# Even projection: the sample group's rows as fp32 products in four PSUM bands, summed by a 0/1 product

## What is computed

```python
def even_mixer(h, pos, R0, w_in, w_out, q_gain, k_gain, attend):
    b, T = h.shape[:2]
    qr, kr, vr, gr, qa, ka, va, qi, ki, wi = _split(h @ w_in, EVEN_SPLITS)
...
def reference(...):
...
        np_ = rmsnorm(xp, norm_mix[l])
        ns_ = rmsnorm(xs, norm_mix[l])
```

## Time and profile before

| | |
|---|---|
| median of three runs | 3229.15 us (3225.47 to 3239.33) |
| the profiled execution, its own time | 3233.79 us |
| its span in the trace | 3231.7 us |
| TensorE busy | 2905.4 us, 90% of the span |
| VectorE busy | 1493.0 us, 46% |
| ScalarE busy | 730.5 us, 23% |
| GpSimd busy | 314.2 us, 10% |
| mean granted clock of TensorE | 0.928 |

### The profile page before, as it was taken

The page is one execution under the profiler, slowest core; times in us unless marked ns, Lnnn a source line. Parts: engine busy times, 40 slices in busy tenths (PEclk is TensorE's granted clock), DMA queues, the critical chain, the costliest instruction groups (busy, mean ns, idle before and its releaser), DMA issues. The chain is left out here.

```text
span 3231.7 us, 38976 instructions
## 1 busy us (share of the span) xinstructions
PE 2905.4 (90%) x16549; PEld 2663.2 (82%) x16549; DVE 1493.0 (46%) x2021; ACT 730.5 (23%) x1166; POOL 314.2 (10%) x287
## 2 busy tenths in 40 slices
PE   8889996638879899999999979958799999999998
PEld 7757775627539899999999979836599999999997
DVE  4789994678313433322332345248423332332333
ACT  3533330235321311111111032132312111111110
POOL 1022222512130100000000010015001000000000
PEclk9989998858989899999999989957699999999999
DMA  5022223143132121121121021010202111112111
GB/s 163 7 87 90 95 73 125 48 141 106 48 123 66 46 59 40 40 60 40 40 59 40 14 44 47 22 33 1 62 21 65 40 53 46 40 43 57 40 40 67
DMA packets 210737, 188.18 MB, mean 58 GB/s; under 512 B 22843, under 2 KB 164415, under 8 KB 210425
## 3 DMA queue, kind: packets, MB, share of 16 engines
q1 hardware_dynamic: 204033, 164.36, 16.9%
q0 software_dynamic: 6528, 21.23, 2.2%
HBM read 152.25 MB, written 33.50 MB: 57 GB/s over the span
## 5 line engine op out<-in xcount | busy, mean ns | idle before, releaser
L1929 DVE TENSOR_TENSOR xt<-ps,xt 128x1056 f32<-128x1056 f32 x176 | 221.0, 1256 | 205.7 <-PE ps L1713 205.7
L1713 PE MATMUL ps<-ffn_high,f_whG 128*128 128x352 f32 x1056 | 230.0, 326 | 13.2 <-DVE ffn_low L1643 7.8
L1713 PE MATMUL ps<-f_hidh,f_whD 128*128 128x352 f32 x1056 | 229.6, 326 | 9.9 <-DVE f_wlD L1908 9.9
L1713 PE MATMUL ps<-ffn_low,f_whG 128*128 128x352 f32 x1056 | 229.1, 325 | 0.0
L1713 PE MATMUL ps<-f_hidh,f_wlD 128*128 128x352 f32 x1056 | 228.9, 325 | 0.0
L1713 PE MATMUL ps<-ffn_low,f_whU 128*128 128x352 f32 x1056 | 228.7, 324 | 0.0
L1713 PE MATMUL ps<-f_hidl,f_whD 128*128 128x352 f32 x1056 | 228.4, 324 | 0.0
L1713 PE MATMUL ps<-ffn_high,f_whU 128*128 128x352 f32 x1056 | 227.8, 324 | 0.0
L1713 PE MATMUL ps<-ffn_high,f_wlG 128*128 128x352 f32 x1056 | 227.6, 324 | 0.0
L1713 PE MATMUL ps<-ffn_high,f_wlU 128*128 128x352 f32 x1056 | 226.6, 323 | 0.0
L728 PE MATMUL ps<-pe_wh,even_high 128*128 128x512 f32 (+1 forms) x504 | 200.2, 397 | 13.3 <-POOL pe_wl L760 13.3
(11 more groups left out here) (538 smaller groups left out, 4837.5 us busy)
## 6 DMA issues: line engine op xcount, KB each, us to landing
pe_w<-in_w_in_even_dram SPq DMA_DIRECT2D x7, 2048.0 KB, 8.3
proj<-pe_out SPq DMA_DIRECT2D x56, 256.0 KB, 2.0
ht_even<-in_w_gate_dram SPq DMA_DIRECT2D x22, 512.0 KB, 5.1
ht_even<-in_w_up_dram SPq DMA_DIRECT2D x22, 512.0 KB, 6.3
ht_even<-in_w_down_dram SPq DMA_DIRECT2D x22, 512.0 KB, 3.9
ht_odd<-in_w_gate_dram SPq DMA_DIRECT2D x22, 512.0 KB, 5.1
ht_odd<-in_w_up_dram SPq DMA_DIRECT2D x22, 512.0 KB, 6.3
ht_odd<-in_w_down_dram SPq DMA_DIRECT2D x22, 512.0 KB, 3.9
```

What stands on the lines that cost most here:

```text
L1713: last = pe.matmul(g.ps[0:out_rows, b0 + c, 0:THIRD], lhs, rhs[:, c * THIRD:(c + 1) * THIRD], start=(first and n == 0), stop=(final and n ...
L1929: dve.tensor_tensor(xv, g.ps[:, 3 * (m % 2):3 * (m % 2) + 3, 0:THIRD], xv, ALU.add).then_inc(added, 1)
```

## The change

The sample rows leave the product of three fp32r passes. For each strip, the 8 slices of the sample rows are multiplied with the gained weights in `pe_w` as plain fp32 products; slice k goes to PSUM band k % 4 (32 partitions each) of one bank, so each band sums two slices. ScalarE copies the whole bank to a new tile `pe_bands`, and one more plain fp32 product with a constant 0/1 matrix (`fold`, 128 by 32, a one where row i and column j have i % 32 = j) adds the four bands into partitions 0 to 31 of the same bank. The ninth unit moves from the last to the third place in the order of a strip; its products are issued between the full units 0 and 1, and the fold between 1 and 2. The load of the next strip's weights also waits for the products of the sample rows. The fp32 tile of the sample columns now lives as long as the halves.

```diff
--- before.py
+++ after.py
@@ -119,6 +119,7 @@
     head = 2 * ((q % 16) // 4) + (q % 32) // 16
     put("head_idx", (head[:, None] == np.arange(IH)[None, :]) * 1.0)
     put("page_row", i[:, None] * 1.0)
+    put("fold", (i[:, None] % NS == np.arange(NS)[None, :]) * 1.0)
 
     cnt = np.stack([1.0 / np.minimum(np.arange(PPAST) + 1, 2 ** (g + 1)) for g in range(4)])
     put("pool_head", np.tile(cnt.reshape(1, -1), (P, 1)))
@@ -198,6 +199,7 @@
                 with ExitStack() as normed:
                     halves(normed, "even", "right")
                     g.inverse = room(normed, "even_inverse", [P, TILES], F32, "right")
+                    g.x_sample = room(normed, "x_sample", [P, KD, NS], F32, "right")
                     g.score = room(att, "score", [P, 6, SEQ])
                     g.score_s = room(att, "score_s", [NS, KEYS])
                     stage_front(g)
@@ -288,7 +290,7 @@
         scaled = relu[:, :, :].rearrange("p s n -> p (s n)")[:, 0:2 * T].rearrange("p (s n) -> p s n", s=2)
         x_last = early[:, 2 * SEQ:4 * SEQ].rearrange("p (k n) -> p k n", k=2)
         x_places = (((0, g.score[:, 0:4, :]),), ((0, g.score[:, 4:6, :]), (2, x_last)))
-        x_sample = g.room(st, "fr_x_sample", [P, KD, NS])
+        x_sample = g.x_sample
         block = st.enter_context(nc.Block())
         key_rows = g.ins["cache_kidx"][0].rearrange("n p d -> (n p) d")
         units = [(t, h) for t in range(2, SMP) for h in range(IH)]
@@ -685,16 +687,25 @@
 
     nc = g.nc
     projected, copied = g.sem("pe_projected"), g.sem("pe_copied")
+    banded, bands_read, folded = g.sem("pe_banded"), g.sem("pe_bands_read"), g.sem("pe_folded")
     w_in, w_rounded, w_split = g.sem("pe_weights"), g.sem("pe_rounded"), g.sem("pe_split")
     stored = g.slot_sems("pe_stored", 4)
     found, replaced = g.sem("pe_found"), g.sem("pe_replaced")
+
+    order = [(m, t) for m in range(EVEN_TM) for t in (0, 1, SMP, *range(2, SMP))]
+    place = {unit: n for n, unit in enumerate(order)}
     with ExitStack() as st:
         w = g.room(st, "pe_w", [P, KD, 512])
         wh = g.room(st, "pe_wh", [P, 2, KD, 512], F32R)
         wl = g.room(st, "pe_wl", [P, 2, KD, 512], F32R)
         out = g.room(st, "pe_out", [P, 4, 512])
+        bands = g.room(st, "pe_bands", [P, 2, 512])
         best = g.room(st, "pe_best", [P, 8])
         block = st.enter_context(nc.Block())
+
+        def tiles_before(m, t):
+
+            return SMP * m + t
 
         @block.sync
         def _(sp):
@@ -703,32 +714,59 @@
                              .rearrange("(k p) n -> p k n", p=P)).then_inc(w_in, 16)
 
             load(0)
-            for n in range(EVEN_TM * TILES):
-                m, t = n // TILES, n % TILES
+            for n, (m, t) in enumerate(order):
                 if t == 0 and m + 1 < EVEN_TM:
                     sp.wait_ge(w_split, KD * (m + 1))
+                    sp.wait_ge(banded, m + 1)
                     load(m + 1)
                 sp.wait_ge(copied, n + 1)
                 sp.dma_start(g.proj[m, t * P:t * P + rows(t), :], out[0:rows(t), n % 4, :]).then_inc(stored[n % 4], 16)
             for slot in range(4):
-                sp.wait_ge(stored[slot], 16 * len(range(slot, EVEN_TM * TILES, 4)))
+                sp.wait_ge(stored[slot], 16 * len(range(slot, len(order), 4)))
 
         @block.tensor
         def _(pe):
+            def free(n):
+                if n >= 8:
+                    pe.wait_ge(copied, n - 7)
+
+            def full(m, t):
+
+                n = place[m, t]
+                free(n)
+                for k in range(KD):
+                    if t == 0:
+                        pe.wait_ge(w_split, KD * m + k + 1)
+                    high, low = (h[:, k, t * P:(t + 1) * P] for h in (g.hh, g.hl))
+                    to = g.ps[:, n % 8, :]
+                    pe.matmul(to, high, wh[:, m % 2, k, :], start=(k == 0), stop=False)
+                    pe.matmul(to, high, wl[:, m % 2, k, :], start=False, stop=False)
+                    last = pe.matmul(to, low, wh[:, m % 2, k, :], start=False, stop=(k == KD - 1))
+                last.then_inc(projected, 1)
+
+            def sample(m):
+
+                n = place[m, SMP]
+                free(n)
+                for k in range(KD):
+                    j = k % 4
+                    last = pe.matmul(g.ps[NS * j:NS * (j + 1), n % 8, :], g.x_sample[:, k, :], w[:, k, :],
+                                     start=(k < 4), stop=(k >= 4))
+                last.then_inc(banded, 1)
+
+            def fold(m):
+
+                pe.wait_ge(bands_read, m + 1)
+                pe.matmul(g.ps[0:NS, place[m, SMP] % 8, :], g.c("fold"), bands[:, m % 2, :], start=True, stop=True
+                          ).then_inc(folded, 1)
+
             for m in range(EVEN_TM):
-                for t in range(TILES):
-                    n = m * TILES + t
-                    if n >= 8:
-                        pe.wait_ge(copied, n - 7)
-                    for k in range(KD):
-                        if t == 0:
-                            pe.wait_ge(w_split, KD * m + k + 1)
-                        high, low = (h[:, k, t * P:t * P + rows(t)] for h in (g.hh, g.hl))
-                        to = g.ps[0:rows(t), n % 8, :]
-                        pe.matmul(to, high, wh[:, m % 2, k, :], start=(k == 0), stop=False)
-                        pe.matmul(to, high, wl[:, m % 2, k, :], start=False, stop=False)
-                        last = pe.matmul(to, low, wh[:, m % 2, k, :], start=False, stop=(k == KD - 1))
-                    last.then_inc(projected, 1)
+                full(m, 0)
+                sample(m)
+                full(m, 1)
+                fold(m)
+                for t in range(2, SMP):
+                    full(m, t)
 
         @block.scalar
         def _(act):
@@ -736,20 +774,30 @@
                 if k == 0:
                     act.wait_ge(w_in, 16 * (m + 1))
                     if m >= 2:
-                        act.wait_ge(projected, TILES * (m - 1))
+                        act.wait_ge(projected, SMP * (m - 1))
                 act.activation(wh[:, m % 2, k, :], w[:, k, :], ACT.Copy, scale=g.gain[:, 0, k:k + 1])
                 act.activation(w[:, k, :], w[:, k, :], ACT.Copy, scale=g.gain[:, 0, k:k + 1]).then_inc(w_rounded, 1)
 
+            def read_bands(m):
+                act.wait_ge(banded, m + 1)
+                if m >= 2:
+                    act.wait_ge(folded, m - 1)
+                act.copy(bands[:, m % 2, :], g.ps[:, place[m, SMP] % 8, :]).then_inc(bands_read, 1)
+
             for k in range(KD):
                 high(0, k)
-            for n in range(EVEN_TM * TILES):
-                m, t = n // TILES, n % TILES
-                act.wait_ge(projected, n + 1)
+            for n, (m, t) in enumerate(order):
+                if t < SMP:
+                    act.wait_ge(projected, tiles_before(m, t) + 1)
+                else:
+                    act.wait_ge(folded, m + 1)
                 if n >= 4:
                     act.wait_ge(stored[n % 4], 16 * (n // 4))
                 act.activation(out[0:rows(t), n % 4, :], g.ps[0:rows(t), n % 8, :], ACT.Copy,
                                scale=g.inverse[0:rows(t), t:t + 1]).then_inc(copied, 1)
-                if t < KD and m + 1 < EVEN_TM:
+                if t == 0:
+                    read_bands(m)
+                if t < SMP and m + 1 < EVEN_TM:
                     high(m + 1, t)
 
         @block.gpsimd
```

## The result

The changed kernel takes 3214.19 us (median of 11 runs, 3211.03 to 3223.18) against 3230.24 us before in the same set: a ratio of 0.9949, with a 95% interval of 0.9939 to 0.9958. The forecast was 19.3 us less; the medians differ by 16.05. The direction and the mechanism were right, and 3.3 us of the gain are missing. The median lies 4.4 us above the 3209.8 of the forecast: those 3.3, and 1.1 because the time before is 3230.24 by eleven runs where three had given 3229.15.

What follows compares the result with a forecast made beforehand. TensorE's stream was taken to bound the stage. -38.6 (removed units) + 7 x 1.72 (bands) + 7 x 0.86 (fold) + 1.0 (switches) + 0.3 (tail) = -19.3 us, from 3229.15 to 3209.8 us; range 3204 to 3215, 8 in 10: 3203 to 3225.

Steps and rivals of the forecast that it cites:

- TensorE's stream sets the stage's end, and each us of it counts: Changed stage: a microsecond off TensorE is one off the kernel, until VectorE's 38.5 us wait is used up.
- The removed unit, 7 x 5.52, and the fold's records, 0.86: TensorE: 7 ninth units of 24 products removed, 38.6 us; one plain fp32 fold added per strip at 0.86 us.
- The bands at 1.72 us: TensorE, per strip: 8 plain fp32 sample products in four bands running at once cost 4 x 0.43 us.
- The half-rate case: Rival: bands overlap but at the front stage's rate, 3.40 us per strip, total 3221.6 us; chance 0.12.
- Switches, 1.0 us in the stage, at most 2.1: TensorE: 14 more changes of stationary width and 7 groups of bands cost 0 to 2.1 us, taken as 1.0.
- the sum by that rule, 2.2 us: Alternative switch cost if changing tiling mode drains TensorE: 0.16 us for each of 14 further switches, instead of 1.0 us.
- The order rival: Rival: TensorE starts products only in program order, so bands take 3.87 us per strip, total 3225 us; chance 0.10.
- The slower rival: Rival: bands do not overlap, 6.88 + 0.86 us per strip against 5.52, total 3246 us; chance 0.07.
- ScalarE's copy: ScalarE: one bank copy per strip, 0.69 us, covered by a full unit before the fold; costed at nothing.
- the late load: SyncE: next strip's weight load issued about 7.2 us into the strip instead of about 1; costed at nothing.
- the seam: Between strips: slice 7 ready 3.48 us in, needed at 4.8; costed at nothing. Rival that it opens: chance 0.07.
- the tail: Stage end: last unit's store is 256 KB, 2.0 us to landing, not 64 KB, 1.7 us; +0.3 us.

Runs made afterwards that it cites:

- a0: The changed kernel run again without any edit: 3214.17 us, ratio 0.9947 to the kernel before, stage 342.14 us.
- e1: Changed kernel with all 8 sample products in band 0, no fold and no copy of the bands: 3245.46 us, ratio 1.0044 to before.
- e4: Changed kernel with each strip's fold moved directly ahead of the next strip's band products, except the last: 3212.27 us, ratio 0.9945 to before.
- e6: Changed kernel with the copied bands split in two halves and folded by two fp32r products of 128 by 32: 3207.54 us, ratio 0.9934 to before.
- e5: Changed kernel with the plain fp32 fold matrix 128 columns wide instead of 32: stage 340.26 us, 3220.34 us in one execution.
- e10: Changed kernel with the plain fp32 fold matrix 96 columns wide: stage 340.03 us, 3216.53 us in one execution.
- e11: Changed kernel with the plain fp32 fold matrix 64 columns wide: stage 342.51 us, 3217.05 us in one execution.
- e3: Changed kernel with the sample products issued band by band instead of interleaved: stage 342.29 us, 3215.01 us in one execution.
- e8: Changed kernel with bands behind unit 3, fold behind unit 4, and the next strip's load later with them: stage 342.09 us, 3219.12 us in one execution.
- e9: Changed kernel with ScalarE making slices 5, 6 and 7 of the next strip behind unit 7's copy: stage 349.84 us, 3218.42 us in one execution.

## Why the prediction was right, and where it fell short

- **TensorE's stream sets the stage's end, and each us of it counts.** Right: over all the kernels run, with stages from 337.2 to 369.8 us, the length follows the sum of the distances on TensorE to about 0.3 us. The medians follow it more loosely. Against before in the same set, a0, e1, e4 and e6 differ by -16.8, +14.5, -18.7 and -23.4 us, and in the stage by -15.9, +11.8, -17.7 and -20.8. That the rest, up to 2.7 us, is scatter of medians of 4 to 6 runs is likely but not shown.
- **The removed unit, 7 x 5.52, and the fold's records, 0.86.** Right.
- **The bands at 1.72 us.** Right. The half-rate case did not occur. The Trainium skill's 2.38 times for three bands (TensorE: Matmul & The Clock Gate, Measured speedup vs the span model) had led to an estimate of 3.2 times for four, and that was too low: 6.98 / 1.86 is 3.75 times. That its time, near 3213 us, came closer to the measured one than mine is luck, since the missing time is at the borders and not in slower bands.
- **Switches, 1.0 us in the stage, at most 2.1.** This is the term that failed, in size and at its upper bound. Measured: 0.34 us per strip at the bands and 0.31 at the fold, 7 x 0.65 = 4.5 us. The 3.5 us above my 1.0 are the distance from 19.3 to 15.86, 3.4. The range held them with 0.8 us to spare (3214.19, its end 3215), because it also allowed for a median that moves. The step that misled me was "does not look like a drain, though both units begin in band 0 there": the products at 482.05 and 482.29 are both fp32r, and e6 against e5, e10 and e11 shows that an fp32r product with 32 columns makes no such switch at all. They could not speak about the rule of the Trainium skill (TensorEngine Tiling, Key Properties). I had the sum by that rule, 2.2 us with a price borrowed from the earlier trace rows; it erred the same way as mine, though less. Its count of 14 switches was half of what it is, 28, since the ninth unit of before had none. Its price, 0.16 us, is what comes out (4.5 / 28), but I had no reason to trust it: the distance in the earlier trace rows contains small fp32 records as well.
- **The order rival (products start in program order only).** It did not happen: 1.86 us where a staircase needs 3.9, and 1.87 in e3 where it needs 5.6. The Trainium skill's sentence on strict program order (TensorE: Matmul & The Clock Gate, What overlaps and what doesn't) does not hold in these traces for the starts of records of different bands.
- **The slower rival.** Its price was right to about 1 us: without overlap and without the fold e1 is 11.8 us slower in the stage, and 7 x 0.86 for the fold would make it 17.9, where I had 16.8. Its condition, no overlap, did not hold.
- **ScalarE's copy, the late load, the seam, the tail.** Costed at 0, 0, 0 and 0.3. Measured: nothing (in e5 the fold starts 0.23 us behind the product ahead, so it does not wait for the copy), nothing (e8), a margin of 1.3 us that is real (e9), and 0.4. The strip of before was 50.01 us long and not 49.7, since a full unit takes 5.56 us and not 5.52; the sum does not rest on it.

## What to carry to other kernels

Few stationary columns are cheap only if several such products run in different PSUM bands at once; then plain fp32 in four bands (1.86 us for 8 products) beats three fp32r passes (5.52 us), and in one band it does not (6.98). Each visit of a 32- or 64-column plain fp32 product in a stream of full-width fp32r ones costs about 0.3 us beside its records. So put such products together, or give a lone one 96 or 128 columns where the wider result has room in PSUM, or do it in fp32r, which needs the operand in two halves. A stream of full-width plain fp32 products around it was not measured. Before a row is held against a cost, check that its instruction has the same type and the same place as the one to be added.

## What was not expected of the hardware

- A plain fp32 product of 128 by 32 or 128 by 64 between fp32r products of 128 by 128 costs 0.3 us more than its records (1.17 and 1.20 us); with 96 or 128 columns it costs 0.86 us flat, and a 128 by 32 product in fp32r costs the usual 0.23.
- With four bands, TensorE starts records out of the order of issue: 16 records sorted by band took 1.87 us, the same as interleaved.
- Four streams from 128 partitions at the 2.4 GHz level run as fast as one: 0.43 us for each record of the fullest band, with one, two or four bands.
